# Sparse attention of a two-block transformer: compressed branch folded into the units of the other two, new order of maxima, exponentials and transposes

## What is computed

```python
def nsa_attention(h, w_q, gate_b, w_o, shared):
    k_cmp, v_cmp, k_slc, v_slc, k_win, v_win = shared
    ...
        sc = jnp.einsum('bqghd,bngd->bghqn', qg, k_cmp).astype(jnp.float32) * scale
        valid_c = cmp_end[None, :] <= t[:, None]
        p_cmp = jax.nn.softmax(jnp.where(valid_c, sc, NEG), axis=-1)
        p_cmp = p_cmp * jnp.any(valid_c, axis=-1)[:, None]
        o_cmp = jnp.einsum('bghqn,bngd->bqghd', p_cmp.astype(v_cmp.dtype), v_cmp)
    ...
        p_sel = jax.nn.softmax(ss.reshape(b, G, HPG, Q_BLOCK, topk * SEL_LEN), axis=-1).reshape(ss.shape)
        o_sel = jnp.einsum('bghqkl,bgqkld->bqghd', p_sel.astype(v_sel.dtype), v_sel)
    ...
        p_w = jax.nn.softmax(jnp.where(valid_w, sw, NEG), axis=-1)
        o_win = jnp.einsum('bghqs,bsgd->bqghd', p_w.astype(v_w.dtype), v_w)
    ...
    out = jnp.einsum('bsch,bschd->bshd', gates.astype(o.dtype), o).reshape(b, s, NSA_HEADS * DH)
    return out @ w_o
```

## Time and profile before

| | us |
|---|---|
| median of 3 runs | 2735.23 |
| profiled execution: time | 2727.23 |
| profiled execution: span on the core | 2725.1 |
| TensorE matmul busy in the span | 2491.4 (91%) |
| VectorE, ScalarE, GpSimd busy | 1331.4, 908.6, 1052.6 |
| TensorE in the stage of the change, 853.36 to 1102.40 | 223.57 of 249.04 |

### The profile page before, as it was taken

One profiled execution on the slowest core, in us unless ns is written; L12 is line 12 of the kernel. 1 busy time (PEld: TensorE's weight loads), 2 busy tenths in 40 slices (PEclk: granted clock), 3 DMA queues, 4 the chain that ended last, 5 costly groups with the idle time before them and its releaser, 6 DMA issues.

```text
span 2725.1 us, 36886 instructions
## 1 busy us (share of the span) xinstructions
PE 2491.4 (91%) x13831; PEld 1935.6 (71%) x13831; DVE 1331.4 (49%) x2001; ACT 908.6 (33%) x1691; POOL 1052.6 (39%) x992
## 2 busy tenths in 40 slices
PE   7999899999998989899999699988999999499996
PEld 5777688887576555688888588878988897344542
DVE  3343344433455555344334466662067641767674
ACT  3444322223112455322223333431145400345452
POOL 7553544443051001644444544434751275311122
PEclk8999999999997787999999899998999899599998
DMA  4111333333241000233331311111210130489997
GB/s 127 55 55 47 101 100 93 97 96 87 68 110 46 1 1 1 77 94 96 96 95 37 89 40 47 40 55 55 85 40 24 32 92 17 141 291 352 357 357 251
DMA packets 267868, 268.50 MB, mean 99 GB/s; under 512 B 13339, under 2 KB 198518, under 8 KB 267750
## 3 DMA queue, kind: packets, MB, share of 16 engines
q1 hardware_dynamic: 262998, 253.91, 29.3%
q0 software_dynamic: 4752, 12.98, 1.9%
HBM read 256.10 MB, written 10.75 MB: 98 GB/s over the span
## 4 chain that ended last, share of the span: by engine, by line
PE 80%; DVE 7%; ACT 4%; DMA 4%; issue 3%; POOL 2%; SPq 1%; POOLq 0%; DVEq 0%; ACTq 0%
PE psum L2552 16%; PE psum L2555 15%; PE psum L2556 15%; PE psum L2244 3%; PE psum L1465 3%; PE psum L2316 2%; PE psum L1303 2%; PE psum L1249 2%; PE psum L1288 2%; PE psum L2382 2%; PE psum L2202 2%; PE psum L881 2%; DMA ring_tile<-in_w_up 1%; PE psum L883 1%; PE psum L2208 1%
## 5 line engine op out<-in xcount | busy, mean ns | idle before, releaser
L2552 PE MATMUL psum<-x_hi,w_hi 128*128 128x264 f32 (+1 forms) x1536 | 526.6, 343 | 36.5 <-DVE x_lo L802 12.1
L2555 PE MATMUL psum<-x_lo,w_hi 128*128 128x264 f32 (+1 forms) x1536 | 516.4, 336 | 0.0
L2627 POOL TENSOR_TENSOR w_lo<-ring_tile,w_hi 128x1024 fp32r<-128x1024 f32 x128 | 307.8, 2405 | 381.1 <-ACT w_hi L2610 379.1
L840 POOL TENSOR_TENSOR w_hi<-ring_tile,one 128x256 fp32r<-128x256 f32 (+1 forms) x288 | 239.4, 857 | 520.6 <-PE psum L2556 463.3
L2552 PEld LDWEIGHTS psum<-x_hi,w_hi 128*128 128x128 f32 x1536 | 293.2, 191 | 74.8 <-issue 36.7
L2556 PE MATMUL psum<-x_hi,ring_tile_lo 128*128 128x264 f32 (+1 forms) x1088 | 340.9, 313 | 0.0
L2555 PEld LDWEIGHTS psum<-x_lo,w_hi 128*128 128x128 f32 x1536 | 293.5, 191 | 29.1 <-issue 1.2
L844 POOL TENSOR_TENSOR ring_tile_lo<-ring_tile,w_hi 128x256 fp32r<-128x256 f32 (+1 forms) x288 | 305.7, 1087 | 8.5
L2833 DVE TENSOR_TENSOR h<-psum,h 128x512 f32<-128x512 f32 x80 | 55.0, 692 | 337.3 <-PE psum L2556 270.1
L2610 ACT ACTIVATE w_hi<-ring_tile 128x1024 fp32r<-128x1024 f32 x128 | 135.0, 1057 | 251.7 <-PE psum L2556 240.9
L2556 PEld LDWEIGHTS psum<-x_hi,ring_tile_lo 128*128 128x128 f32 x1088 | 207.6, 191 | 11.8
(11 more groups left out here) (411 smaller groups left out, 5107.9 us busy)
## 6 DMA issues: line engine op xcount, KB each, us to landing
ring_tile<-in_mlp_w SPq DMA_DIRECT2D x128, 512.0 KB, 3.9
ring_tile<-in_w_gate SPq DMA_DIRECT2D x64, 512.0 KB, 7.3
ring_tile<-in_w_up SPq DMA_DIRECT2D x64, 512.0 KB, 7.2
ring_tile<-in_w_down SPq DMA_DIRECT2D x64, 512.0 KB, 7.7
ring_tile<-in_w_in SPq DMA_DIRECT2D x52, 512.0 KB, 3.9
ring_tile<-in_sb_w_qkv SPq DMA_DIRECT2D x24, 512.0 KB, 3.8
ring_tile<-in_nsa_w_kv SPq DMA_DIRECT2D x12, 512.0 KB, 3.6
ring_tile<-in_sb_w_o SPq DMA_DIRECT2D x8, 512.0 KB, 3.6
```

What stands on the lines that cost most here:

```text
L840: last = pool.tensor_tensor(hi[:, cols], raw[:, cols], one[:, :].broadcast_to([P, D // len(parts)]), ALU.mult)
L2552: upper = pe.matmul(dst, a_hi, b_hi, start=first, stop=False)
L2555: pe.matmul(dst, a_hi, b_lo, start=False, stop=False)
L2627: pool.tensor_tensor(lo, raw, hi.bitcast(F32), ALU.subtract).then_inc(split_w, 1)
```

## The change

There are 16 units, selected and window of each pair. The compressed branch is no unit any more: its steps are placed inside the others, with buffers of its own (`cmp_T`, `cmp_s`) in place of shares in `probs_T`, `top` and `rsum`.

- Its scores go into one of the two fill banks (5 or 6) in place of banks 0 and 1. The 8 products on half the rows become 4 on all 128 rows: `k_both` holds the pair's keys once for each head, in 62 columns, with zeros in the other head's rows. A memset and two copies replace the copy of `k_cmp`.
- `PIECES` become two, `((3,), (1, 2, 0))`. In the second, products of tile 1 of one head stand beside products of tile 2 of the other head, and the six masks come at the end.
- VectorE takes all maxima of unit `d + 1` ahead of the scaling of unit `d`, and each maximum raises `ns_m` by itself.
- ScalarE takes all exponentials of unit `d + 1` (and the compressed one) ahead of the five takes of unit `d`.
- TensorE weighs in two halves, tiles 0 and 2 after take 3, tiles 1 and 3 after take 4. In selected units a compressed fill stands ahead of the last fill, another between the two halves, and the compressed weighing behind them. Fill 3 stands ahead of the second score piece in selected units and behind it in window units.
- `slot_taken` makes a TensorE instruction that writes bank 5 or 6 wait for the reader of what was there two slots earlier.

The diff, cut:

```diff
-UNITS = NSA_PAIRS * BRANCHES
+UNITS = 2 * NSA_PAIRS
...
-        k_cmp = at("k_cmp", [P, GROUPS, N_CMP], STAGE_AT + 40960)
+        k_both = at("k_both", [P, GROUPS, 2 * N_CMP], XN_AT + 7168)
...
+        cmp_T = at("cmp_T", [P, 2, SEQ], XN_AT)
         cmp_p = at("cmp_p", [P, 2, QT, N_CMP], XN_AT + 6144)
+        cmp_s = at("cmp_s", [P, 2, QT], XN_AT + 7136)
...
-            dve.tensor_copy(k_cmp[:, :, :].rearrange("p g n -> p (g n)"), bank[0][:, 0:GROUPS * N_CMP])
+            step(dve, dve.memset(k_both[:, :, :], 0.0))
+            for hh in range(2):
+                dve.tensor_copy(k_both[HALF[hh], :, N_CMP * hh:N_CMP * hh + N_CMP],
+                                bank[0][HALF[hh], 0:GROUPS * N_CMP].rearrange("p (g n) -> p g n", g=GROUPS))
...
-        PIECES = ((3,), (2, 0), (1,))
...
+        PIECES = ((3,), (1, 2, 0))
+        MAX_AT = {3: 1, 1: 2, 2: 4, 0: 4}
...
+        def slot_bank(s):
+            return bank[5 + s % 2]
+
+        def slot_taken(pe, s):
+
+            was = s - 2
+            if was < 0:
+                return
+            u = (was + 3) // SLOTS_PER_PAIR
+            if was == 0 or (was == cmp_slot(u) and u < NSA_PAIRS):
+                pe.wait_ge(cmp_blk, cmp_no(u if was else 0))
+            else:
+                pe.wait_ge(ns_t, was - min((was + 2) // SLOTS_PER_PAIR, NSA_PAIRS - 1))
...
+            if k == 0:
+                for n in range(3):
+                    for hh in range(2):
+                        product(3, hh, n)
+                mask(3, 0)
+                mask(3, 1).then_inc(ns_s, 1)
+                return
+            for n in range(3):
+                last = product(1, 0, n)
+                if n == 2:
+                    last.then_inc(ns_s, 1)
+                product(2, 1, n)
+            for n in range(3):
+                product(2, 0, n)
+                if n == 0:
+                    pe.wait_ge(ns_s, score_no(d, 0) + 1)
+                product(1, 1, n)
+            for n in range(3):
                 for hh in range(2):
-                    for n, (a, b) in enumerate(products):
-                        product(1, hh, a, b, n == 0)
-                    last = mask(1, hh)
-                    if hh == 0:
-                        last.then_inc(ns_s, 1)
-                        pe.wait_ge(ns_s, score_no(d, k))
-            else:
-                for i in PIECES[k]:
-                    for n, (a, b) in enumerate(products):
-                        for hh in range(2):
-                            product(i, hh, a, b, n == 0)
-                    for hh in range(2):
-                        last = mask(i, hh)
+                    product(0, hh, n)
+            for i in (2, 1, 0):
+                for hh in range(2):
+                    last = mask(i, hh)
             last.then_inc(ns_s, 1)
 
+        def cmp_scores(pe, u):
+            dst = slot_bank(cmp_slot(u))
+            slot_taken(pe, cmp_slot(u))
+            for i in range(QT):
+                last = pe.matmul(dst[:, 2 * 32 * i:2 * 32 * i + 2 * N_CMP], q_raw[:, u, i * P:(i + 1) * P], k_both[:, u // 2, :],
+                                 start=True, stop=True)
+            last.then_inc(cmp_mm, 1)
...
+            for k in range(2):
+                nsa_scores(pe, 0, k)
+            nsa_scores(pe, 1, 0)
+            cmp_scores(pe, 0)
+            nsa_scores(pe, 1, 1)
+            for d in range(UNITS):
+                u, slc, more = d // 2, d % 2 == 0, d + 2 < UNITS
+                nsa_fill(pe, d, 0)
+                nsa_fill(pe, d, 1)
+                if more:
+                    nsa_scores(pe, d + 2, 0)
+                if not slc and more:
+                    cmp_scores(pe, u + 1)
+                nsa_fill(pe, d, 2)
+                if slc:
+                    nsa_fill(pe, d, 3)
+                if more:
+                    nsa_scores(pe, d + 2, 1)
+                if slc:
+                    cmp_fill(pe, u, 0)
+                else:
+                    nsa_fill(pe, d, 3)
+                nsa_fill(pe, d, 4)
+                pe.wait_ge(ns_t, fill_at(d, 3) + 1)
+                if slc and u:
+                    pe.wait_ge(ns_oe, u)
+                nsa_weigh(pe, d, (0, 2))
+                if slc:
+                    cmp_fill(pe, u, 1)
+                pe.wait_ge(ns_t, fill_at(d, 4) + 1)
+                last = nsa_weigh(pe, d, (1, 3))
+                if slc:
+                    cmp_weigh(pe, u)
+                else:
+                    last.then_inc(ns_o, 1)
...
+                act.wait_ge(ns_m, 4 * d + MAX_AT[i])
...
+            for k in range(2):
+                nsa_exps(act, 0, k)
+            for d in range(UNITS):
+                u, slc, more = d // 2, d % 2 == 0, d + 1 < UNITS
+                if more:
+                    nsa_exps(act, d + 1, 0)
+                if slc:
+                    cmp_exps(act, u)
+                if more:
+                    nsa_exps(act, d + 1, 1)
+                for k in range(4):
+                    nsa_take(act, d, k)
+                if slc:
+                    cmp_take(act, u, 0)
+                nsa_take(act, d, 4)
+                if slc:
+                    cmp_take(act, u, 1)
...
-                last = dve.reduce_max(top[:, b, :, i], both_banks(i), AX.X, negate=True)
-            last.then_inc(ns_m, 1)
+                dve.reduce_max(top[:, d % 2, :, i], both_banks(i), AX.X, negate=True).then_inc(ns_m, 1)
...
+            for k in range(2):
+                nsa_maxima(dve, 0, k)
             for d in range(UNITS):
-                todo = list(range(len(pieces((d + 1) % BRANCHES)))) if d + 1 < UNITS else []
-                for k in todo[0:2]:
-                    nsa_maxima(dve, d + 1, k)
+                u, slc, more = d // 2, d % 2 == 0, d + 1 < UNITS
+                if not slc:
+                    cmp_normalise(dve, u)
+                    if u:
+                        nsa_out(dve, u - 1)
+                if more:
+                    nsa_maxima(dve, d + 1, 0)
+                if slc:
+                    cmp_softmax(dve, u)
+                if more:
+                    nsa_maxima(dve, d + 1, 1)
                 nsa_normalise(dve, d)
-                for k in todo[2:]:
-                    nsa_maxima(dve, d + 1, k)
-                if d and d % BRANCHES == 0:
-                    nsa_out(dve, d // BRANCHES - 1)
             nsa_out(dve, NSA_PAIRS - 1)
```

More of the change, by code:

```diff
@@ L31 @@
 GROUPS = 4
-BRANCHES = 3
 NSA_PAIRS = 8
-UNITS = NSA_PAIRS * BRANCHES
+UNITS = 2 * NSA_PAIRS
 CMP_LEN, CMP_STRIDE, CMP_HID = 32, 16, 256
@@ L1292, in nsa_weigh @@
-        def nsa_weigh(pe, d):
-            u, br = d // BRANCHES, d % BRANCHES
-            pe.wait_ge(ns_t, fill_no(d, len(fills(br)) - 1))
-            if br == 0:
-                if u:
-                    pe.wait_ge(ns_oe, u)
-                for hh in range(2):
-                    pe.matmul(bank[7][HALF[hh], :], v_cmp[:, u // 2, :], probs_T[0:N_CMP, hh, 0:SEQ], start=True, stop=False, skip_group_check=True)
-                return
-            for j in range(QT):
+            if k == 0:
[5 more added lines that the diff above has]
+                return
@@ new lines, in nsa_scores, with cmp_fill @@
+            last.then_inc(ns_s, 1)
+        def cmp_scores(pe, u):
[5 more added lines that the diff above has]
+            last.then_inc(cmp_mm, 1)
+        def cmp_fill(pe, u, hh):
+            f = cmp_fill_at(u, hh)
+            slot_taken(pe, fill_slot(f))
+            pe.wait_ge(cmp_hh, cmp_no(u))
+            for i in range(QT):
+                last = pe.transpose(slot_bank(fill_slot(f))[0:N_CMP, i * P:(i + 1) * P], cmp_p[:, hh, i, :], ident[:, :])
+            last.then_inc(ns_tt, 1)
@@ new lines, in nsa_fill, with nsa_weigh @@
+        def nsa_fill(pe, d, k):
+            f = fill_at(d, k)
+            slot_taken(pe, fill_slot(f))
+            pe.wait_ge(ns_f, head_no(d, 0 if k < 2 else 1))
+            at = 0
+            for hh, j in FILLS[k]:
+                for i in range(j, QT):
+                    last = pe.transpose(slot_bank(fill_slot(f))[:, at:at + P], probs[d % 2][hh][:, PROB_AT[i] + j * P:PROB_AT[i] + (j + 1) * P], ident[:, :])
+                    at += P
+            last.then_inc(ns_tt, 1)
+        def nsa_weigh(pe, d, js):
+            u, br = d // 2, 1 + d % 2
+            for j in js:
@@ L1304, in nsa_weigh, with cmp_weigh @@
                                      probs_T[:, hh, PT_AT[j]:PT_AT[j] + CAUSAL_COLS[j]],
-                                     start=False, stop=(br == 2 and j == QT - 1), skip_group_check=True)
-            if br == 2:
-                last.then_inc(ns_o, 1)
+                                     start=(br == 1 and j == 0), stop=(br == 2 and j == QT - 1), skip_group_check=True)
+            return last
+        def cmp_weigh(pe, u):
+            pe.wait_ge(ns_t, cmp_fill_at(u, 1) + 1)
+            for hh in range(2):
+                pe.matmul(bank[7][HALF[hh], :], v_cmp[:, u // 2, :], cmp_T[0:N_CMP, hh, :], start=False, stop=False, skip_group_check=True)
```

(1 more changed line is left out.)

168 lines of the change are left out of this document (65 added, 103 removed).

## The result

The kernel after takes 2664.81 us (median, 2662.75 to 2671.24) against 2733.62 for the kernel before (median of 4 runs, 2728.07 to 2737.54): a ratio of 0.9754, 95% interval 0.9729 to 0.9778. The profiled execution took 2662.75 with a span of 2660.6, 64.5 us less than the one of before. The forecast was 2701, the range 2672 to 2730; the measured time is that of rival 1, 2663.

What follows compares the result with a forecast made beforehand. The prediction took TensorE and its clock to bound the stage. A pair at 27.1 against 30.9 us saves 3.8, times 8 pairs 30, less 0.7 for the memset: -30 from 2731 gives 2701, range 2672 to 2730.

Steps and rivals of the forecast that it cites:

- rival 1: In the changed stage the clock stays up with no fall; 68 us less, 2663 in all; chance 0.12.
- What bounds the kernel: The changed stage, 249.0 us, is bound by TensorE, busy 223.6, and by its clock, mean 0.74.
- Formula: A pair lasts s + (1 - s / 38.4) x 21.2 + idle, s being time at the lower clock level.
- Score piece: Second score piece with tiles of both heads overlapped: 2.46 in place of 3.09 us at clock 1.00, 0.63 a unit gained.
- Compressed scores and moves at zero: Compressed scores on all rows taken as 0, between -0.9 and +0.1; compressed fills, weighing and takes moved, 0.
- Memset: Memset and two copies replacing one copy ahead of the query projections: +0.7 us once, between 0.3 and 1.2.
- Idle: TensorE's idle is moved, not removed: 2.5 us a pair, as much as before.
- Start and end: First and last iterations of the stage: between -3 and +3 us in total, taken as 0.
- The clock: TensorE's clock still falls once a pair, at an idle of about 1.1 us amid compressed scores and sparse score piece.
- long stretches at 1.00: Sign in the stage's profile after that would make the prediction wrong on the lower side.
- Time at the lower level after a fall: In each pair TensorE spends 10.5 us at the lower clock level, between 7 and 14.
- Rival 4: ScalarE's late takes hold TensorE back in every unit, lower clock becomes normal; +22 us, 2753; chance 0.11.

Runs made afterwards that it cites:

- e1: Kernel before, with the two ScalarE takes of the compressed unit moved behind the selected unit's second exponential piece; 2698.95 us, 0.9893 of the kernel before.
- e3: Kernel after, with three small ScalarE activations into an unused tile added ahead of the takes of window units; 2679.89 us, 0.9814 of the kernel before.
- e10: Kernel after, with the compressed weighing moved from the selected unit's end to behind the window unit's compressed scores; 2690.56 us, 0.9839 of the kernel before.
- e11: Kernel after, with six small ScalarE activations added ahead of the takes of window units, in place of e3's three; 2690.45 us, 0.9838 of the kernel before.
- e4: Kernel after, with tile 1 of the second score piece again done one head after the other; 2678.17 us, 0.9821 of the kernel before.
- e9: Kernel before, with the compressed branch left out of the attention stage, its output missing from the result; 2653.50 us, 0.9699 of the kernel before.
- e6: Kernel after, with VectorE's scaling of a unit moved ahead of the next unit's second piece of maxima; 2662.70 us, 0.9751 of the kernel before.
- e7: Kernel after, with ScalarE's first two takes moved between the next unit's exponentials of tile 1 and of tiles 2 and 0; 2656.09 us, 0.9719 of before.
- e5: Kernel after, with the edits of e3 and e4 together; 2690.93 us, 0.9871 of the kernel before.

## Why the prediction was wrong

- *What bounds the kernel*: right. TensorE and its clock; the other engines' busy time is the same after.
- *Formula*: right. 0.45 us of stage for each us at the lower level together with the change in waits accounts for e1, e3, e10 and e11 within about 2 us.
- *Score piece*: the mechanism was right, the size was not. Products of unequal length do overlap on the two row halves; the piece takes 1.86, not 2.46: the mixed tiles 1.14 (928.62 to 929.76), where I had 1.44, and tile 0 with the six masks 0.72 (to 930.48), where I had 1.02. e4 gives 13 us for it where 0.63 x 16 = 10 stood.
- *Compressed scores and moves at zero*: right. 0.94 for four full-row products at clock 1.00 is what half of 1.92 gives. In sum, a pair has 18.6 of work (21.1 less 2.5 of idle), nearly the 19.9 of the prediction less the 1.2 by which two score pieces came out shorter.
- *Memset*: 0.7 forecast; the copy of `v_cmp` behind it starts 0.8 later. (Where the stage starts shows nothing on this: in kernels with the same code ahead of it that varies from 851.37 to 854.70.) Rows of DVE, before and after:

```profile
796.22 0.40 DVE L1079 COPY v_cmp<-psum 31x256 f32<-31x256 f32 x1
```
```profile
797.04 0.41 DVE L1083 COPY v_cmp<-psum 31x256 f32<-31x256 f32 x1
```
- *Idle*: right in total. In the stretch at 1.00 it is 17.5 in 150.2 us, 2.5 a pair, most of it in the places named; at the third fill it is 0.6, not 1.1.
- *Start and end*: I took 0 in -3 to +3. The steady pairs gained 8 x (30.0 - 21.1) = 71, the stage 64: start and end cost 7 more. Part of it is the first fill, which waits 3.6 for VectorE (the longest of the waits above), and 6.8 us at the lower level near the end.
- *The clock*: this is the step that failed. I took "one fall a pair" because an idle of about 1.1 amid sparse work "looks like the one at which it falls now". The idle was 1.0, and no fall came: no time at the lower level in the 150.2 us of the middle, where 10.5 a pair stood. The falls of before hung on the compressed unit as a whole, a thin iteration with a wait of 1.4 in it: without the unit there are none (e9), without that wait there are fewer and shorter ones (e1), and in the kernel after it took waits of 1.9 to 2.9 to bring them back (e3, e10, e11), those of 1.9 not always. Rival 1 named this, "work is evened out, no iteration is thin", with a chance of 0.12, and long stretches at 1.00, given as the sign of a prediction wrong on the lower side, are what the profile shows. That its 2663 is so near the measured 2664.81 is luck: two errors met, a score piece that was 0.6 a unit better (some 10 us) and a start and end that were 7 us worse.
- *Time at the lower level after a fall*: 10.5 taken, 3.4 in the falls of e3, in e10 3.4 in five, once 6.8 and once 10.2. These stand at the same wait in iterations of the same instructions; the five of 3.4 us began 2.3 to 3.0 us behind the end of the wait, the two longer ones within 0.5 us of it. I had let the lower level last through score piece, transposes and weighing; in e3 the clock was back amid the score piece. So this step was wrong too, and why a fall begins and ends where it does stays open.
- *Rival 4*: no sign of it. Pairs with 48 transposes in 21.1 us ran at 1.00 throughout, which fits that transposes stood ahead of a rise; no stretch of transposes alone is long enough here to show more.

So the 64.3 us divide as follows, by three kernels in a row: 31.8 from taking the wait out of the thin iteration by moving two takes (before to e1), 19.5 from spreading the compressed branch, with all the new orders (e1 to e4), 13.0 from the score piece (e4 to after). In the second step the lower level fell by 41 us, at 0.45 18 of the 19.5. In another order of steps the shares could come out otherwise; that wasn't tried. Of the new orders the clock doesn't need VectorE's (e6), nor all exponentials ahead of the takes (e7); TensorE's order and the weighing in two halves weren't undone by themselves.

What stays open is what makes the clock fall at one wait of 1.9 and not at the next, with the same instructions around it (e3). A longer wait brought more falls (of seven waits of 1.0, 1.9 and 2.9 us in the kernel after, e3 and e11: 0, 5 and 7, but of 1.9 in e5 only 1), and sparse work nearly without a wait came ahead of some (e1), but these two don't decide the single case. Whether the moment at which the wait comes does was not tested, and with one profile for each kernel the counts of falls are those of one execution.

## What to carry to other kernels

When TensorE's clock moves in a stage, read the stage as iterations and look for the thin one: here a short unit between long ones left a wait without cover, and its cost was the wait plus 0.45 of the time at the lower level that followed. Moving two small instructions of another engine out of the way was worth three times the wait that is seen (31.8 against 10.6), and evening out the work another 19.5. Count the falls in several executions before you compare two kernels by them. Before adding cover in front of a wait, check that the engine that ends the wait doesn't itself wait for that cover.

## What the runs showed of the hardware that I had not expected

- A fall of the clock can last 3.4 us or 17.1 (3.4 and 10.2 within e10, at the same wait), and waits of 1.0 us in each pair left the clock at 1.00 for 150 us, while those of 2.9 did not. The Trainium skill (TensorE: Matmul & The Clock Gate, Part 1, "HAM oscillation") tells of a kernel whose clock goes down at a wait for DMA in every turn of its loop. The traces agree that a wait can do this turn after turn: e10 and e11 do. But here it is a wait for ScalarE, and those before which falls came, 2.0 and 2.9 us, are shorter than those of the page's example.
- Products on the two row halves of the array overlap also when they are of unequal length (256 beside 384 columns): tiles 1, 2 and 0 of both heads take 1.86 with their masks, 2.79 with tile 1 serial (e4).
- Two kernels with equal instructions outside a stage differ there by up to 11 us of 2480 in their profiled executions. A gain of 10 us is better read from the stage than from the total.
